# Low halves of attention queries as two 64-row matmuls on separate row groups

## The reference

```python
DIFF_HEADS, DIFF_DH, Q_BLOCK = 4, 64, 128
q = q.reshape(B_, T, DIFF_HEADS, 2, DIFF_DH)
k = k.reshape(B_, T, DIFF_HEADS, 2, DIFF_DH)
for i in range(T // Q_BLOCK):
    L = (i + 1) * Q_BLOCK
    qb = q[:, i * Q_BLOCK:L]
    s = jnp.einsum('bqhmd,bkhmd->bhmqk', qb, k[:, :L]) * scale
    mask = jnp.arange(L)[None, :] <= (i * Q_BLOCK + qpos)[:, None]
    p = jax.nn.softmax(jnp.where(mask, s, NEG), axis=-1)
    a = p[:, :, 0] - lam_full * p[:, :, 1]
    outs.append(jnp.einsum('bhqk,bkhe->bqhe', a, v[:, :L]))
```

## Time and profile before

| what | value |
|---|---|
| three timed runs | 2414.78, 2415.39, 2415.46 us |
| median of them | 2415.39 us |
| span of the profiled execution | 2412.4 us |
| PE busy | 2249.7 us (93%) |
| DVE busy | 1481.6 us (61%) |
| mean granted clock of PE | 0.971 |
| first attention stage, scores of pieces | 257 to 485 us |
| second attention stage, scores of pieces | 1122 to 1537 us |

### The profile page before, as it was taken

How to read it: one execution, slowest core, us unless ns; L and a number is a source line. 1 busy time by engine, 2 the same in 40 slices (tenths; PEclk the granted TensorE clock), 3 DMA queues, 4 the chain that set the end, 5 groups by cost and what they waited for, 6 DMA issues and landing times. The chain is left out here.

```text
span 2412.4 us, 35099 instructions
## 1 busy us (share of the span) xinstructions
PE 2249.7 (93%) x11572; PEld 1862.3 (77%) x11572; DVE 1481.6 (61%) x2645; ACT 1121.4 (46%) x2386; POOL 849.3 (35%) x739
## 2 busy tenths in 40 slices
PE   3698999998999999998999999999999978899998
PEld 3586788887777778786888888878888856787886
DVE  6675777857888885313766667445555436375671
ACT  4553566645445444323666566433434334344351
POOL 1223333335566563200222223123424306363453
PEclk7899999999999999999999999999999989999999
DMA  7699888768877777988565655497877775465561
GB/s 265 245 360 352 280 256 271 246 240 307 271 249 260 254 246 273 344 260 271 166 182 172 176 175 166 152 288 233 248 243 245 221 262 214 156 235 191 186 228 61
DMA packets 344859, 569.98 MB, mean 236 GB/s; under 512 B 31472, under 2 KB 217200, under 8 KB 339824
## 3 DMA queue, kind: packets, MB, share of 16 engines
q1 hardware_dynamic: 310416, 443.04, 54.5%
q10 hardware_dynamic: 34272, 124.80, 16.4%
HBM read 336.53 MB, written 236.45 MB: 238 GB/s over the span
## 5 line engine op out<-in xcount | busy, mean ns | idle before, releaser
L1765 PE MATMUL gb<-h_hi,w_both 128*128 128x512 f32 x1904 | 786.6, 413 | 65.2 <-DVE o L1301 34.2
L1767 PE MATMUL gb<-h_hi,w_both 128*128 128x512 f32 x1904 | 755.3, 397 | 0.0
L1766 PE MATMUL gb<-h_lo,w_both 128*128 128x512 f32 x1904 | 753.7, 396 | 0.0
L1765 PEld LDWEIGHTS gb<-h_hi,w_both 128*128 128x128 f32 x1904 | 364.9, 192 | 149.6 <-issue 75.7
L1767 PEld LDWEIGHTS gb<-h_hi,w_both 128*128 128x128 f32 x1904 | 364.1, 191 | 80.8
L1766 PEld LDWEIGHTS gb<-h_lo,w_both 128*128 128x128 f32 x1904 | 366.0, 192 | 66.7
L996 ACT ACTIVATE o<-gb 128x512 f32<-128x512 f32 x272 | 161.7, 595 | 377.5 <-PE gb L1767 316.1
L860 POOL TENSOR_TENSOR C_prob<-C_prob,C_cf 128x512 f32<-128x512 f32 (+3 forms) x160 | 160.5, 1028 | 465.5 <-DVE C_cf L1409 461.3
L1061 ACT ACTIVATE C_prob<-C_sc,C_negm 128x512 f32<-128x512 f32 (+3 forms) x320 | 198.7, 622 | 223.5 <-DVE C_negm L1387 212.7
L1301 DVE TENSOR_TENSOR o<-gb,o 128x512 f32<-128x512 f32 x204 | 140.1, 687 | 225.4 <-PE gb L1767 214.0
L1291 DVE TENSOR_TENSOR w_both<-w,w_both 128x512 fp32r<-128x512 f32 x170 | 151.0, 889 | 106.7 <-ACT w_both L973 106.2
(11 more groups left out here) (235 smaller groups left out, 3752.9 us busy)
## 6 DMA issues: line engine op xcount, KB each, us to landing
wS_scratch<-w_both SPq DMA_DIRECT2D x238, 512.0 KB, 3.9
w_both<-wS_scratch ACTq DMA_DIRECT2D x238, 512.0 KB, 4.3
w<-in_w_in_dram SPq DMA_DIRECT2D x68, 512.0 KB, 5.5
gT_scratch<-o SPq DMA_DIRECT2D x128, 256.0 KB, 4.7
D_gate<-gT_scratch SPq DMA_DIRECT2D x32, 1024.0 KB, 4.9
pT_scratch<-o SPq DMA_DIRECT2D x80, 256.0 KB, 4.4
D_wm_stage<-wm_scratch SPq DMA_DIRECT2D x32, 640.0 KB, 6.0
C_qt<-qB_scratch SPq DMA_DIRECT2D x128, 128.0 KB, 3.5
```

Source lines behind the costliest of these rows:

```text
L1765: mm(to, hi[:, k, :], h_hi[j][:, k, :], start=(fresh and k == 0), stop=False, skip_group_check=True)
L1766: mm(to, hi[:, k, :], h_lo[j][:, k, :], start=False, stop=False, skip_group_check=True)
L1767: last = mm(to, lo[:, k, :], h_hi[j][:, k, :], start=False, stop=(k == KH - 1), skip_group_check=True)
```

## The change

The scores of one piece had two matmuls over 128 partitions per map: high queries times (high keys, low keys), and low queries times (high keys, low keys). The product low times low goes out. What is left of the second matmul, low queries times high keys, needs only 64 partitions. The keys of map 1 are stored and loaded the other way round, so that the high keys of map 0 lie on partitions 0 to 63 and those of map 1 on partitions 64 to 127. The tile `qt` shrinks from four to three pieces: high queries of map 0 and of map 1 on both halves, and one piece with the low queries of map 0 on the lower half and of map 1 on the upper half. `load_q` issues three DMAs instead of two. `scores(z)` now issues the high matmuls of both maps, then two matmuls over 64 partitions each, on different row groups and into different banks, then the two masks.

```diff
-            qt = [sb(f"qt{j}", [P, 2, 2, P], F32R) for j in range(QT)]
+            qt = [sb(f"qt{j}", [P, 3, P], F32R) for j in range(QT)]
...
-                    sp.dma_start(kT[col - 24, 0, :, t:t + TG], hb[x][:, :]).then_inc(hb_stored[x], 16)
-                    sp.dma_start(kT[col - 24, 1, :, t:t + TG], o[b][:, :]).then_inc(o_stored[b], 16)
+                    sp.dma_start(kT[col - 24, :, 0, :, t:t + TG], hb[x][:, :]).then_inc(hb_stored[x], 16)
+                    sp.dma_start(kT[col - 24, :, 1, :, t:t + TG], o[b][:, :]).then_inc(o_stored[b], 16)
...
-                for part in range(2):
+
+                blocks = kT[head, :, :, :, g * TG:(g + 1) * TG].rearrange("m l d t -> d (m l) t")
+                for part, pair in enumerate((slice(0, 4, 3), slice(1, 3))):
                     sp.dma_start(ks[DH * part:DH * part + DH, :, g * TG:(g + 1) * TG].bitcast(F32),
-                                 kT[head, part, :, g * TG:(g + 1) * TG].rearrange("(m d) t -> d m t", m=2)).then_inc(k_loaded[g], 16)
+                                 blocks[:, pair, :]).then_inc(k_loaded[g], 16)
...
-                    sp.dma_start(qt[i % QT][DH * part:DH * part + DH, :, :, :].rearrange("d l m t -> d (l m) t").bitcast(F32),
-                                 qB[head, y].rearrange("l m d t -> d (l m) t")).then_inc(q_loaded[i % QT], 16)
+                    sp.dma_start(qt[i % QT][DH * part:DH * part + DH, 0:2, :].bitcast(F32),
+                                 qB[head, y, 0].rearrange("m d t -> d m t")).then_inc(q_loaded[i % QT], 16)
+                sp.dma_start(qt[i % QT][:, 2, :].bitcast(F32), qB[head, y, 1].rearrange("m d t -> (m d) t")).then_inc(q_loaded[i % QT], 16)
...
-                    pe.wait_ge(q_loaded[i % QT], 32 * (i // QT + 1))
+                    pe.wait_ge(q_loaded[i % QT], 48 * (i // QT + 1))
+                queries = qt[i % QT]
+                keys = ks[:, :, p * TG:p * TG + w]
+                banks = [sc[(2 * z + m) % 3][:, 0:w] for m in range(2)]
                 for m in range(2):
-                    q = 2 * z + m
-                    if q >= 3:
-                        pe.wait_ge(exp_done, q - 2)
-                    bank = sc[q % 3]
-                    mm(bank[:, 0:w], qt[i % QT][:, 0, m, :], ks[:, m, p * TG:p * TG + w], start=True, stop=False)
-                    last = mm(bank[:, 0:w], qt[i % QT][:, 1, m, :], ks[:, m, p * TG:p * TG + w], start=False, stop=True)
-                    if z == begin[i]:
-                        last = mm(bank[:, w - P:w], ident_r[:, :], causal_r[:, :], start=False, stop=True,
-                                  skip_group_check=True)
-                    last.then_inc(s_ready, 1)
+                    if 2 * z + m >= 3:
+                        pe.wait_ge(exp_done, 2 * z + m - 2)
+                    mm(banks[m], queries[:, m, :], keys[:, m, :], start=True, stop=False, skip_group_check=True)
+                for m in range(2):
+                    rows_m = slice(DH * m, DH * m + DH)
+                    last = mm(banks[m], queries[rows_m, 2, :], keys[rows_m, m, :], start=False, stop=True, skip_group_check=True)
+                    if z != begin[i]:
+                        last.then_inc(s_ready, 1)
+                if z == begin[i]:
+                    for m in range(2):
+                        mm(banks[m][:, w - P:w], ident_r[:, :], causal_r[:, :], start=False, stop=True,
+                           skip_group_check=True).then_inc(s_ready, 1)
```

More of the change, by code:

```diff
@@ L2363, in hybrid_trunk @@
     qB = nc.dram_tensor("qB_scratch", [HEADS, NT, 2, 2, DH, P], F32).ap()
-    kT = nc.dram_tensor("kT_scratch", [HEADS, 2, P, T], F32).ap()
+    kT = nc.dram_tensor("kT_scratch", [HEADS, 2, 2, DH, T], F32).ap()
     vT = nc.dram_tensor("vT_scratch", [T, HEADS * P], F32).ap()
```

## The result

| | median | lowest to highest | runs |
|---|---|---|---|
| before | 2415.43 us | 2414.78 to 2419.82 | 4 |
| after | 2548.22 us | 2547.19 to 2548.96 | 4 |

The ratio is 1.0549, 95% interval 1.0536 to 1.0562: 133 us slower. The forecast was slower as well, but by 25 us. The sign was right, and some four fifths of the loss (108 of 133 us) were not in the sum.

The account below looks back on a forecast made before the run. The prediction took PE to bound the kernel in the attention stages. Saved matmul slots -32.2, shape switches +54.4 and waits on the exponentials +3 gave +25 on 2415.4, so 2440 us, range 2415 to 2456.

Parts of the forecast that it names:

- the paragraph on the loads: DMAs on SP: third query load and exchanged map-1 keys cost nothing, since SP has room and loads run ahead.
- one of the prediction's own signs: Changed kernel's timeline: PE stays fully busy in both attention windows; a 512-wide piece takes 1.02 to 1.04 us.
- PE sets the pace: Attention stages: PE busy 199.9 of 200 and 300.0 of 300 us, so its cost goes into time almost one to one.
- Pairs run side by side, -32.2 us: Scores on PE: the two 64-row matmuls run together, three slots per piece instead of four, 32.2 us off PE.
- Rival C: Scores on PE: the pair is not concurrent in float32r, 32.2 us more, 2472 us; chance 0.08.
- Into the pair, 0.14 us: PE's switch from full 128-row matmuls to the 64-row pair: 0.09 + 0.05 = 0.14 us a piece.
- Out of the pair, 0.20 us: PE's switch from the pair back to full matmuls, weight load not hidden: 0.20 us a piece.
- The sum on PE: All 160 pieces: 54.4 us of switches at 0.34 each against 32.2 us saved, leaving 22.2 us.
- The wait on the exponentials, +3: PE's second `exp_done` wait: 14 stalls, 0.23 us extra at each, taken as +3 us, between 0 and 8.
- the later maxima, 0: DVE's maxima: map 0 ready after 0.83 us instead of 0.46, DVE idle up to 0.37 us a piece, costed at nothing.
- The third query DMA, 0: SP's loads: one more issue of 0.61 us per unit, 20 us of SP's time in each stage, costed at nothing.
- Rivals A and B: A: shape switches on PE cost nothing, 2383 us, chance 0.10. B: only one switch is paid, 2415 us, chance 0.08.

Follow-up runs that it names:

- the old store: Changed kernel with keys stored and laid out as before, map 1's swap made in the load, 64-row pair kept: 2442.45 us, ratio 1.0099.
- the serial version: Kernel with the old store, both low matmuls on partitions 0 to 63 so they cannot run side by side: 2472.02 us, ratio 1.0227.
- the experiment with three full slots: Kernel with the old store, one full 128-row matmul in place of the pair, map 0's low product left out: 2394.46 us, ratio 0.9899.
- The order alone: Kernel before with high matmuls of both maps, then low ones, then masks, all over 128 rows: 2417.08 us, ratio 1.0003.
- the two entries: Kernel with the old store, map 0's low matmul moved between the two high ones, entering the 64-row shape twice per piece: 2533.32 us, ratio 1.0486.

## Why the prediction was wrong, and where it was right

**The step that failed** is a sentence in the paragraph on the loads: "The exchanged map-1 keys change addresses, not the number or size of the rows", with the verdict "All this at nothing". Number and size of the rows were indeed the same. But the paragraph on loads speaks of the load only, which keeps 64 rows in front, and nowhere of the store, whose 128 rows fell apart into 2 times 64. The kernel before plus this one edit is 108 us slower. The diff showed it in two lines: an index went from `[.., 0, :, ..]` to `[.., :, 0, :, ..]`. The queue was looked at for its issue time, 0.6 us, from rows of other shapes; the issue of the low keys' store takes 5.0 us at the median in the new shape, that of the high keys' 0.66.

None of the rivals held this either. They were all about PE. And the range, 2415 to 2456, had no room for a transfer going wrong. One of the prediction's own signs shows it: PE was to stay fully busy in the windows of the earlier trace rows. In the changed kernel it is busy 187.3 of 200 and 282.7 of 300 us, with the old store 200.0 and 299.6.

**The rest of the sum, step by step:**

- *PE sets the pace.* Right for work added in the attention stages: a slot of 32 us gave 30, a slot and a second entry, 86 us at my price and 96 at the measured 0.40, gave 91. Only partly right for work taken away: 32 us gave 23, the next 32 about 13; the reason is open.
- *Pairs run side by side, -32.2 us.* Right that they do; the serial version cost 30 us more. Rival C is out.
- *Into the pair, 0.14 us.* Too small. In float32r, with rows of the kernel with the old store:

```profile
1335.21 0.62 PE L1835 MATMUL C_sc<-C_ks,C_qt 128*128 128x512 f32 x2
1335.76 0.50 PE L1838 MATMUL C_sc<-C_ks,C_qt 64*128 64x512 f32 x2
```

The second high matmul ends at 1335.83 and the pair at 1336.26, 0.43 apart, which is 0.20 over the usual 0.23; the median over the 112 pieces with 512 keys is 0.43 as well. The start is 0.32 after the last full one as forecast; what grew is the part behind it, the pair's records being 0.11 longer than a full matmul's 0.39 where those of the earlier trace rows were 0.05 longer than their like.
- *Out of the pair, 0.20 us.* Right. In the changed kernel the pair ends at 1340.34, the two value matmuls at 1340.76, so the first of them 0.11 earlier at 1340.65: 0.31, against 0.11 for such a matmul in a dense row. By starts the piece takes 0.98 us (1339.29 to 1340.27) and not the 1.02 to 1.04 of the prediction's signs, since much of the price of leaving lies behind the next start.
- *The sum on PE.* 0.40 us a piece instead of 0.34: 160 x 0.40 - 32.2 = +32 instead of +22. The span of the kernel with the old store is 2443.6, 31 over before's 2412.4; by medians of the timed runs it is 25 (20 to 28), which is below the new sum, and the 7 us between them are open. Forecast: +25.
- *The wait on the exponentials, +3, and the later maxima, 0.* The 14 stalls were misread: the earlier trace rows puts matmuls and weight loads together, and PE's matmuls waited at L1831 only 6 times, 3.2 us in all, as the row in the experiment with three full slots shows. That makes +1 in place of +3, by the same 0.23. The order alone measured 0 within 3 us, with the old store PE waited 5 times, 3.1 us, and DVE's idle time on the maxima rose as thought without PE waiting for it. For the earlier trace rows, the kernel with the old store:

```profile
  PE C_sc L1838: 68.1, 50
```

It was 47.5 us in 35 cases, and is 68.1 in 50, 0.13 us a piece and not the 0.37 at most.
- *The third query DMA, 0.* Right as far as it was tried: it is also in the two kernels without the pair, which are faster than before, and it was not taken out alone.

Rivals A and B are out by the two entries, where 160 more entries and exits cost 59 us against A's 0 and B's 32, and by the rows above, which show a price in both directions. Without the store the forecast of 2440 us would have stood against 2442.5 and 2442.9 measured; that the total landed there with the switches 10 us too small, the waits up to 3 too large and some 7 us unplaced is partly luck.

## What to carry to other kernels

When a layout changes, write down for every DMA that touches it, store and load, the list of dimensions after merging, and compare the leading one: a leading 2 in place of 128 cost more here than all the arithmetic that was moved. Cutting such a transfer along that dimension, or moving the odd stride to the side that already has 64 rows in front, makes it harmless.

A lone pair of 64-row matmuls among full ones saves one slot (0.23 us at 512 columns) and pays 0.30 to 0.40 us for entering and leaving, by whether it is taken from the difference of kernels or from the timeline; by these numbers it would pay only where several pairs stand together, which was not tried. And here an engine that was 100% busy paced the time in full for work added, and only in part for work taken away.

## What the runs showed of the hardware beyond that

- One slow store does not only finish late. The issuing queue itself is held: in the first jump the issues of the low keys' stores, and of the weight stores behind them, took 5 to 9 us where their medians in the kernel before are 0.43 and 0.33. The sixteen DMA engines together fell to 0.13 of their time, two engines' worth, over 6 us at a time.
- Sixteen such pairs of stores in the whole kernel, 8 MB of 566 MB moved, cost 108 us, 6.7 us for each pair (32 stores of 256 KB).
- The stalls took PE's granted clock to 0.59 to 0.63 over 18 to 19 us, so part of the jumps is paid by the first matmuls after them (those at 124.17, 124.60 and 125.03 us start 0.43 us apart instead of 0.23).
- A pair of float32r matmuls on 64 rows has records 0.50 us long at 512 columns, where a full one has 0.39; both members start within 0.01 us.
